# The low parts of 43 weight slabs formed by adding DMAs, bias rows read without a mirrored product, and a regrouped first chain

## What is computed

```python
h = rms_norm(x, attn_norm_g[l])
proj = h @ w_in[l]          # hq, hf, hi, hg, cq, ak, av, ik, iw, gate_a, gate_b
oa = hgrn2_mixer(hq, hf, hi, lbs[l])            # recurrence, 4 heads of 128
cq = rms_norm(cq, q_norm_g[l])
aq = cq @ w_uq[l];  iq = cq @ w_iq[l]           # queries of attention and of the index
ob = dsa_mixer(aq, iq, iw, ak, av, ik, rel_bias) # scores + rel_bias[bucket(distance)], 8 heads
mix = sigmoid(gate_a) * (oa @ w_up_hgrn[l]) + sigmoid(gate_b) * (ob @ w_up_attn[l])
x = x + mix @ w_o[l]
x = x + square(relu(rms_norm(x, mlp_norm_g[l]) @ w_mlp_in[l])) @ w_mlp_out[l]
out = rms_norm(x, final_norm_g)
```

## Time and profile before

| | |
|---|---|
| median of 3 runs | 743.09 us (742.93 to 743.39) |
| the profiled execution: its time / its span | 743.21 us / 741.4 us |
| PE busy | 724.2 us, 98% |
| DVE, ACT, POOL busy | 531.5, 358.8, 101.0 us |
| granted TensorE clock | 0.997 of full |

### The profile page before, as it was taken

One profiled execution on the slowest core, in us unless ns is written; L12 is line 12 of the kernel. 1 busy time (PEld: TensorE's weight loads), 2 busy tenths in 40 slices (PEclk: granted clock), 3 DMA queues, 4 the chain that ended last, 5 costly groups with the idle time before them and its releaser, 6 DMA issues.

```text
span 741.4 us, 9808 instructions
## 1 busy us (share of the span) xinstructions
PE 724.2 (98%) x3498; PEld 605.1 (82%) x3498; DVE 531.5 (72%) x805; ACT 358.8 (48%) x576; POOL 101.0 (14%) x128
## 2 busy tenths in 40 slices
PE   5999999999999999999999999999999999999996
PEld 4788878888788888888888888888888888888885
DVE  4676998888799873336634696867768595968964
ACT  6463544765643555543313754545363554545442
POOL 6021240014431354200200100000000000000002
PEclk9999999999999999999999999999999999999998
DMA  7422122120422111112622333241505041332002
GB/s 295 145 84 86 57 90 82 58 85 30 143 85 83 61 57 57 57 58 85 255 86 76 152 114 114 86 142 57 170 8 194 24 156 70 113 114 85 30 1 113
DMA packets 20723, 71.50 MB, mean 96 GB/s; under 512 B 2344, under 2 KB 3536, under 8 KB 20688
## 3 DMA queue, kind: packets, MB, share of 16 engines
q1 hardware_dynamic: 19120, 67.88, 26.2%
q10 hardware_dynamic: 1568, 3.15, 1.2%
HBM read 68.91 MB, written 2.11 MB: 96 GB/s over the span
## 4 chain that ended last, share of the span: by engine, by line
PE 92%; DVE 3%; ACT 2%; DMA 1%; issue 1%; SPq 0%; POOL 0%; POOLq 0%; DVEq 0%; ACTq 0%
PE bank L1492 28%; PE bank L1494 27%; PE bank L1493 27%; PE bank L1500 2%; PE bank L1722 2%; PE bank L1623 2%; DMA xs<-x 1%; PE bank L1704 1%; PE bank L1703 1%; PE bank L1674 0%; PE bank L1635 0%; PE bank L1688 0%; DVE wlo L1000 0%; PE bank L1613 0%; PE bank L1614 0%
## 5 line engine op out<-in xcount | busy, mean ns | idle before, releaser
L1492 PE MATMUL bank<-hTh,whi 128*128 128x512 f32 (+1 forms) x456 | 182.4, 400 | 1.7 <-DVE hTl L1020 1.3
L1494 PE MATMUL bank<-hTh,wlo 128*128 128x512 f32 (+1 forms) x456 | 177.8, 390 | 0.0
L1493 PE MATMUL bank<-hTl,whi 128*128 128x512 f32 (+1 forms) x456 | 177.7, 390 | 0.0
L1492 PEld LDWEIGHTS bank<-hTh,whi 128*128 128x128 f32 (+1 forms) x456 | 85.4, 187 | 21.5 <-issue 4.2
L1494 PEld LDWEIGHTS bank<-hTh,wlo 128*128 128x128 f32 (+1 forms) x456 | 85.2, 187 | 18.5
L1493 PEld LDWEIGHTS bank<-hTl,whi 128*128 128x128 f32 (+1 forms) x456 | 85.4, 187 | 17.9 <-issue 1.0
L1000 DVE TENSOR_TENSOR wlo<-raw,whi 128x1024 fp32r<-128x1024 f32 x51 | 66.0, 1296 | 31.6 <-ACT whi L674 31.5
L674 ACT CAST whi<-raw 128x1024 fp32r<-128x1024 f32 x58 | 60.4, 1043 | 40.9 <-PE bank L1494 40.6
L1492 PE MATMUL bank<-whi,ah 128*128 128x512 f32 x196 | 76.2, 389 | 0.0
L1493 PE MATMUL bank<-wlo,ah 128*128 128x512 f32 x196 | 76.2, 389 | 0.0
L1494 PE MATMUL bank<-whi,al 128*128 128x512 f32 x196 | 76.2, 389 | 0.0
(11 more groups left out here) (233 smaller groups left out, 1380.0 us busy)
## 6 DMA issues: line engine op xcount, KB each, us to landing
raw<-slabs SPq DMA_DIRECT2D x87, 512.0 KB, 3.3
br<-slabs SPq DMA_DIRECT2D x32, 512.0 KB, 3.3
xs<-x SPq DMA_DIRECT2D x4, 512.0 KB, 5.5
y<-x ACTq DMA_DIRECT2D x1, 2048.0 KB, 8.6
out<-ys SPq DMA_DIRECT2D x3, 512.0 KB, 2.6
bt<-bias_rows ACTq DMA_DIRECT2D x1, 1024.0 KB, 6.9
cst<-consts SPq DMA_DIRECT2D x1, 608.0 KB, 9.1
fg<-final_g SPq DMA_DIRECT2D x1, 512.0 KB, 7.1
```

The lines of the kernel that those rows point to most:

```text
L1492: pe.matmul(dst, lh, rh, start=start, stop=False)
L1493: pe.matmul(dst, lh, rl, start=False, stop=False)
L1494: return pe.matmul(dst, ll, rh, start=False, stop=stop)
```

## The change

**Low parts by DMA.** For slabs 4 to 46 ACT writes, right behind the high copy, its negative into `wlo` (one more instruction of 128x1024, which waits for the copy), and POOL issues a DMA that adds `raw` onto it (L648 of the changed kernel). PE's wait for the slab and SP's load into the place wait for that DMA. The low parts of slabs 0, 2, 3 and 47 on stay on DVE, that of slab 1 goes to POOL, ahead of the masks `mskb`, which also wait for the low part of slab 2. POOL's issue for slab n + 2 stands at the head of its list for slab n.

**Bias rows.** The DRAM rows are written 128 times over, by ACT's queue at slab 4 (1.57 MB), and read back with a step that needs no mirroring; `flip` and its copies are gone.

**First chain.** The square of the last input tile is halved, ACT taking one half and DVE the other; the scaling of that tile is halved too, and PE starts its transposes after the first. `hi(1)` moves between the fourth and fifth `hTh`. In feature-major products the order becomes high-high, low-high, high-low, and PE waits for `hTh` alone ahead of the first two.

The diff, cut to its core:

```diff
-        scratch = nc.dram_tensor("bias_rows", [AH, BT_LEN], F32).ap()
+        scratch = nc.dram_tensor("bias_rows", [AH, P, BT_LEN], F32).ap()
...
-        BY_POOL = range(n_uq + 1, n_ua + 1)
-        NLO = NPLAN - len(BY_POOL)
+        BY_DMA = range(n_hf+4, n_wo)
+        NLO = NPLAN - len(BY_DMA) - 1
...
+            pool.wait_ge(hi_done, 2)
+            pool.tensor_tensor(wlo[1][:, :], raw[1][:, :], whi[1][:, :].bitcast(F32), ALU.subtract).then_inc(S["lo1_done"], 1)
+            pool.wait_ge(lo_done, 2)
...
                     if u == 0:
-                        b, n_ = BK["flip", AH // 2 - 1][0]
-                        pool.wait_ge(free[b], n_ + 1)
+                        pool.wait_ge(S["bt_in"], 16)
...
+            def split_by_dma(n):
+
+                if n in BY_DMA:
+                    s = n % SLOTS
+                    pool.wait_ge(S["neg_done"], n - BY_DMA[0] + 1)
+                    pool.dma_start(wlo[s][:, :].bitcast(F32), raw[s][:, :], accum_op=ALU.add).then_inc(lod_done[s], 16)
+
             for n in range(NPLAN):
-                if n + AHEAD in BY_POOL:
-                    q = (n + AHEAD) % SLOTS
-                    pool.wait_ge(hi_done, n + AHEAD + 1)
-                    pool.tensor_tensor(wlo[q][:, :], raw[q][:, :], whi[q][:, :].bitcast(F32),
-                                       ALU.subtract).then_inc(lop_done, 1)
+                split_by_dma(n - 1 + AHEAD)
...
                 act.copy(whi[s][:, :], raw[s][:, :]).then_inc(hi_done, 1)
+                if n in BY_DMA:
+                    act.wait_ge(hi_done, n + 1)
+                    act.activation(wlo[s][:, :], whi[s][:, :].bitcast(F32), ACT.Copy, scale=-1.0).then_inc(S["neg_done"], 1)
...
-            hi(1)
+                if k == 3:
+                    hi(1)
...
-                if k == "flip":
-                    h = s[1]
-                    b, u = BK[s][0]
-                    wait_full((b, u))
-                    act.activation(bt[:, 512 * h:512 * h + 512], bank[b][:, :], ACT.Copy).then_inc(free[b], 1)
...
+            dve.wait_ge(x_in[3], 16)
+            h_ = xs3[:, 3, D // 2:D]
+            dve.tensor_tensor_reduce(rt[0][:, :], h_, h_, 1.0 / D, EPS, ALU.mult, ALU.add,
+                                     ssx[:, NT:NT + 1]).then_inc(S["sqd_done"], 1)
+            xn(2, slice(0, D))
...
-            lo(1)
...
-                    if p == LO_PART[n] and n + AHEAD not in BY_POOL:
+                    if p == LO_PART[n] and n + AHEAD not in BY_DMA:
                         lo(n + AHEAD)
...
                 for k in (k0, k0 + 1):
+                    if rounded is not None:
+                        pe.wait_ge(S[rounded], k + 1)
+                    dst = bank[b][:, 0:T - t0]
+                    pe.matmul(dst, wh[:, k, c0:c0 + P], hi_[:, k, t0:T], start=k == 0, stop=False)
+                    pe.matmul(dst, wl[:, k, c0:c0 + P], hi_[:, k, t0:T], start=False, stop=False)
                     if split_of is not None:
                         pe.wait_ge(free[split_of[k][0]], split_of[k][1] + 1)
-                    ins = three(bank[b][:, 0:T - t0], wh[:, k, c0:c0 + P], wl[:, k, c0:c0 + P], hi_[:, k, t0:T],
-                                lo_[:, k, t0:T], k == 0, k == kt - 1)
+                    ins = pe.matmul(dst, wh[:, k, c0:c0 + P], lo_[:, k, t0:T], start=False, stop=k == kt - 1)
...
-                if k == "flip":
-
-                    h = s[1]
-                    b, u = BK[s][0]
-                    pe.wait_ge(S["bt_in"], 16)
-                    wait_free((b, u))
-                    pe.matmul(bank[b][:, :], flip, bt[:, 512 * h:512 * h + 512], start=True, stop=True).then_inc(full[b], 1)
```

More of the change, by code:

```diff
@@ L158, in build @@
         mskb = place("mskb", 205.5, LEVELS * 64)
-        ssx, rsx = small[:, 0:4], small[:, 4:8]
+        ssx, rsx = small[:, 250:255], small[:, 4:8]
         ssq, rsq = small[:, 8:12], small[:, 12:16]
@@ L378, in build @@
         BY_COUNT = seen
-        BY_POOL = range(n_uq + 1, n_ua + 1)
-        NLO = NPLAN - len(BY_POOL)
+        BY_DMA = range(n_hf+4, n_wo)
+        NLO = NPLAN - len(BY_DMA) - 1
         def split_done(n):
-            if n in BY_POOL:
-                return lop_done, n - BY_POOL[0] + 1
-            return lo_done, n + 1 - sum(m in BY_POOL for m in range(n))
+            if n == 1:
+                return S["lo1_done"], 1
+            if n in BY_DMA:
+                return lod_done[n % SLOTS], 16 * len([m for m in BY_DMA if m <= n and m % SLOTS == n % SLOTS])
+            return lo_done, n + 1 - sum(m in BY_DMA or m == 1 for m in range(n))
         def used_up(n):
@@ L573, in _ @@
                 pool.wait_ge(S["sq_done"], SQ_X + t + 1)
-                rsqrt_mean(rsx[:, t:t + 1], ssx[:, t:t + 1], 1, D).then_inc(S["rs_done"], 1)
+                ss = ssx[:, t:t + 1]
+                if t < NT - 1:
+                    chain(pool.tensor_scalar(ss, ss, 1.0, EPS, ALU.mult, ALU.add))
+                else:
+                    pool.wait_ge(S["sqd_done"], 1)
+                    chain(pool.tensor_tensor(ss, ss, ssx[:, NT:NT + 1], ALU.add))
+                pool.tensor_tensor(rsx[:, t:t + 1], ss, mhalf[:, 0:1], ALU.pow).then_inc(S["rs_done"], 1)
+            pool.wait_ge(hi_done, 2)
+            pool.tensor_tensor(wlo[1][:, :], raw[1][:, :], whi[1][:, :].bitcast(F32), ALU.subtract).then_inc(S["lo1_done"], 1)
+            pool.wait_ge(lo_done, 2)
             chain(pool.memset(mskb[:, :], 1.0))
@@ L689, in _ @@
                 act.wait_ge(x_in[t], 16)
-                square(xs3[:, t, :], D, ssx[:, t:t + 1])
+                w = D if t < NT - 1 else D // 2
+                square(xs3[:, t, 0:w], w, ssx[:, t:t + 1], D ** -0.5)
             hi(0)
@@ L794, in do_side @@
                                    scale=DH ** -0.5).then_inc(free[b], 1)
+                if k == "rows_out":
+                    b, u = BK["bias_rows",][0]
+                    act.wait_ge(free[b], u + 1)
+                    act.dma_start(scratch, rbias[:, :].unsqueeze(1).to_broadcast([AH, P, BT_LEN])).then_inc(S["scr_done"], 16)
                 if k == "log":
@@ L1004, in wait_full, with xn @@
                 dve.wait_ge(full[bu[0]], bu[1] + 1)
-            for t in range(NT):
+            def xn(t, of):
                 dve.wait_ge(S["rs_done"], t + 1)
-                dve.tensor_scalar(xs3[:, t, :], xs3[:, t, :], rsx[:, t:t + 1], None,
-                                  ALU.mult).then_inc(S["xn_done"], 1)
+                dve.tensor_scalar(xs3[:, t, of], xs3[:, t, of], rsx[:, t:t + 1], None, ALU.mult).then_inc(S["xn_done"], 1)
+            xn(0, slice(0, D))
+            xn(1, slice(0, D))
+            dve.wait_ge(x_in[3], 16)
[3 more added lines that the diff above has]
+            xn(2, slice(0, D))
+            dve.wait_ge(S["sqd_done"], 1)
+            xn(3, slice(0, D // 2))
+            xn(3, slice(D // 2, D))
             lo(0)
             dve.wait_ge(vec_in, 16)
-            dve.tensor_tensor(lbd, vec[:, V_LB0:V_LB0 + 4], vec[:, V_LB1:V_LB1 + 4],
-                              ALU.subtract).then_inc(S["lbd_done"], 1)
-            dve.tensor_scalar(ghg, vec[:, V_HG:V_HG + 4], 0.5, None, ALU.mult).then_inc(S["ghg_done"], 1)
             def lo_scaled(dst, bu, scale, hi_ap, hi_sem, val):
@@ L1506, in _ @@
                 for k in range(KD_):
+                    if t == NT - 1 and k == KD_ // 2:
+                        pe.wait_ge(S["xn_done"], NT + 1)
                     ins = pe.transpose(bank[k][:, t * P:(t + 1) * P], xs3[:, t, k * P:(k + 1) * P], ident)
@@ L1559, in mms @@
                     feature_part(tiles[n][0], 2 * p, hTh3, hTl3, slab_view(whi, s, KD_), slab_view(wlo, s, KD_), KD_, 0,
-                                 [(k, 0) for k in range(KD_)] if n == 0 else None)
+                                 [(k, 0) for k in range(KD_)] if n == 0 else None, 0, "hTh_done" if n == 0 else None)
                 elif kind in ("iq", "uq"):
```

27 lines of the change are left out of this document (14 added, 13 removed).

## The result

The changed kernel takes 751.71 us (median of 4, 751.0 to 752.88), the kernel before 743.14. The ratio is 1.012, with a 95% interval of 1.0108 to 1.0132: slower by 8.6 us where 0.8 was forecast, and outside the range given. Its profiled execution has a span of 749.3 us, 7.9 more than before.

The account below looks back on a forecast made before the run. PE was taken to bound the kernel, busy 724.2 of 741.4 us. Terms -3.48 - 0.33 - 0.24 + 2.40 + 1.09 + 1.35 = +0.79 on 743.21 gave 744.0 us, range 740.2 to 747.5.

Parts of the forecast that it names:

- the sentence on the bias rows: DRAM write at slab 4 and read at 185 us: over 100 us between them, so no cost.
- The adding DMAs themselves: Adds into `wlo` from slab 4 on: landing in 3.3 to 8.6 us, about 5, so likeliest no cost.
- The margins of the adds: Time from issue to PE's need: 8.0 us at slab 4, 8.8 to 9.9 at slabs 24 to 26, steady about 13.
- Rival 2: Adds land late, PE waits at slabs 4 and 24 to 26: 8.2 us, so 752; chance 0.14.
- Mirrored products: Near 195 us, four mirrored products of the bias rows vanish from PE: a gain of 3.48 us.
- The index stage: From 130 to 147 us, negations of slabs 20 to 22 delay `iqs` and `hKT`: a cost of 2.40 us.
- `aqs`, +1.09: Slab 24, near 192 us: a negation ahead of `aqs` is paid in full, a cost of 1.09 us.
- The attention's start: Before 233 us, PE waits for mask steps in units 2 and 3: a cost of 1.35 us.
- the relief of 0.24: DVE's low part at 253.61, ahead of a mask step PE awaits, goes: a gain of 0.24 us.
- DVE's queue: Ahead of the attention, DVE's queue with top-k rounds is only 1.13 us shorter than the shift given it.
- The ACT block it feared: At the attention's start, a negation now behind the copy that ACT's exponential of unit 1 follows by 0.17 us.
- The first chain: Near 15 to 21 us, PE's wait for the low part of slab 1 goes: a gain of 0.33 us.

Follow-up runs that it names:

- the run with the small write: Changed kernel with the 8 bias rows formed in reversed order, written once (12 KB), and POOL reading `bt` backwards: 741.55 us, ratio 0.9985.
- the four bare negatives: Kernel with small write, new first chain and adds for slabs 28 to 46, plus four unused ACT negatives (slabs 20, 21, 22, 27): 742.17 us, ratio 0.9998.

## Why the prediction was wrong, step by step

**The step that failed** is the sentence on the bias rows: "The larger DRAM write (1.57 MB at slab 4) and the read at 185 us have over 100 us between them [...]: nothing." It asked only whether the write is done in time for its reader. It did not ask what else is in the DMA engines meanwhile, and the change itself had put 43 transfers there whose landing PE waits for. The step beside it, "The adding DMAs themselves: nothing, in the likeliest case", failed with it: the add of slab 7 took 22.0 us where the range ended at 8.6. The write took some 48 us. What was put at nothing cost +8.6 at slab 7 and +1.0 at 91 us, where ACT had been held up by two late loads; the run with the small write has neither, and the difference of the medians is 10.2 (9.9 within the groups).

**The margins of the adds** used the right landing: the median of 5.0 lies where it was put. But each was compared with a plain transfer on quiet engines. The trace of before could have warned: the slab loads there land in 3.3 us, the input tiles, several at once, in 5.5. Slab 4's margin was also read off a wrong row: ACT's copy at 27.25 is that of slab 5 and not the first for an adding DMA. Slab 4's in the kernel before:

```profile
23.15 1.04 ACT L674 CAST whi<-raw 128x1024 fp32r<-128x1024 f32 x1
```

It changed nothing: POOL's masks were the later condition, POOL issued the adds for slabs 4 and 5 together at 28.8 (near 30 was said), and both were in time.

**Rival 2, adds that land late,** gave 752 and had 0.14. Its number is right and its cause is not. It named waits at slabs 4 and 24 to 26 and DVE's grip on what it shares with POOL; the stall was at slab 7, and it went when one write was changed, with DVE just as busy (for 12.1 of the 16 us from 40 to 56 in the changed kernel, and for 12.2 with the small write). That the time came out near this rival is luck. Adds issued while DVE is busiest, and then in the quieter stretch behind, land like this (medians):

```profile
wlo<-raw POOLq DMA_DIRECT2D x7, 512.0 KB, 6.1
...
wlo<-raw POOLq DMA_DIRECT2D x8, 512.0 KB, 4.6
```

6.1 against 4.6 us, and the 1 MB read of the bias rows runs in the first stretch as well. So what the Trainium skill, "SBUF — State Buffer", section "SBUF: two separate sides", says of DVE and descriptors accounts for at most 1.5 us of a median landing here, and PE waits for no DMA in either stretch.

**Mirrored products, -3.48:** measured -3.6, from +11.88 to +8.28.

**The index stage, +2.40:** measured +2.3 (8.52 to 10.81), with the waits for `iqs` 1.08, `rel` 0.55 and `hKT` 1.03 against 0.61 before. The size is right and so is the cause, which the four bare negatives show by themselves. The places differ a little: "about 1 more for `hKT`" was 0.4, and the wait for `rel` was not named.

**`aqs`, +1.09:** measured +1.08.

**The attention's start, +1.35, and the relief of 0.24:** forecast +1.1 together, measured -0.4, and PE has no wait in the attention's first units, where above 1 us was to be seen. The mechanism was real: without the adds it costs 3.0, more than was said. The term that was mis-sized is DVE's queue, "only 1.13 shorter [...] (one low part gone)". DVE's first mask step moved from 226.78 to 235.45, by 8.67, while `aqs` moved by 11.88: so the queue was 3.2 shorter. The low part is 1.13 of that; the rest is the `hO` steps, which no longer have POOL's low parts beside them. Before, then after:

```profile
200.27 6.43 DVE L1270 SCALAR_TENSOR_TENSOR hO<-hO,small,hSG 128x128 f32<-128x128 f32 x16
...
212.13 4.29 DVE L1291 SCALAR_TENSOR_TENSOR hO<-hO,small,hSG 128x128 f32<-128x128 f32 x16
```

The prediction had seen DVE and POOL slow each other down, but used it only against the adds. The ACT block it feared left no wait. Here the two parts of the change need each other: without the adds, the mirrored products' removal brings 1.1 of its 3.5.

**The first chain, -0.33:** the profiled execution shows -1.09, two kernels side by side show nothing. It lies within what the arrival of the input moves, so the -1.1 in the sum below is mostly chance.

**The sum of the parts** is -1.1 + 8.6 + 1.0 + 2.3 + 1.1 - 3.6 - 0.4 = 7.9, the difference of the spans. Without the two terms of the write it is -1.7, where the forecast had +0.8.

What stays open: how much of the write's slowness is the source in 8 partitions and how much its order, and why its packets hold an engine for longer.

## What to carry over

A transfer that has all the time in the world for itself is not free if others beside it are awaited: ask of every large DMA how long it will occupy the engines, from how many partitions it comes, and what lands meanwhile. When an engine's work is handed to a DMA, the ring gets a second landing for each slab, and its lead covers the sum of both. Matmuls taken away just ahead of an engine that is already full mostly move the wait, so relieve that engine in the same stretch, and count what another engine's instructions beside it cost it; here adds for 19 slabs in place of 43 gave 738.5 us, 4.4 below the kernel before.

## What the runs showed of the hardware

- An adding DMA of 512 KB within SBUF, issued by POOL, takes 4.5 us at best from issue to landing, 5.0 in the median, and its issue occupies POOL for 0.87 us. A plain load of the size takes 3.3.
- A write of 1.57 MB to DRAM in 1536-byte packets took some 33 us from 8 partitions without adds beside it, 48 with them, and 16.6 us, with them, from a copy in DRAM in another order. Beside the slow one, loads of 512 KB took up to 20.5 us (17.5 without adds) and adds up to 24.6.
- A pause of 7 us of PE brought the granted clock from 1.00 to 0.50, and with the restart about 1.6 us more were lost beside the pause itself.
- Sixteen DVE steps of 128x128 took 4.29 us where POOL made no low part beside them, and 5.93 to 6.43 where it did; POOL's low parts, mostly 2.4 us, took up to 3.63 there.
- POOL reading an operand backwards showed no cost: 0.73 us for its `bm` step in the median (kernel before with the small write), 0.74 forwards.
